# Down projections of four feed-forward blocks by Strassen's identity, as a stage behind gate and up

## The reference

```
def swiglu(x, w_gate, w_up, w_down):
    return (jax.nn.silu(x @ w_gate) * (x @ w_up)) @ w_down
...
x = layer_norm(alpha * x + 0.5 * swiglu(x, ffn_w_gate[l, 0], ffn_w_up[l, 0], ffn_w_down[l, 0]), ln_g[l, 0], ln_b[l, 0])
```

## Time and profile before

| | |
|---|---|
| median of 3 runs | 2386.46 us (2380.72 to 2388.42) |
| profiled execution, its own time | 2380.86 us |
| its span, first to last instruction | 2378.9 us |
| granted TensorE clock, mean of the span | 0.913 |
| busy PE, DVE, ACT, POOL | 1944.8, 363.2, 220.1, 17.3 us |
| first FFN matmul at | 1143.8 us |

### The profile page before, as it was taken

How to read it: one execution, slowest core, us unless ns; L and a number is a source line. 1 busy time by engine, 2 the same in 40 slices (tenths; PEclk the granted TensorE clock), 3 DMA queues, 4 the chain that set the end, 5 groups by cost and what they waited for, 6 DMA issues and landing times.

```text
span 2378.9 us, 20900 instructions
## 1 busy us (share of the span) xinstructions
PE 1944.8 (82%) x9324; PEld 1227.4 (52%) x9324; DVE 363.2 (15%) x785; ACT 220.1 (9%) x423; POOL 17.3 (1%) x41
## 2 busy tenths in 40 slices
PE   6987566665666665665999999999999999989997
PEld 5755222222222222221677777777677767857775
DVE  1213111111011111100100032200120015240002
ACT  4231000000000000000100010100010002110000
POOL 1100000000000000000000000000000000000000
PEclk9999878888888888777999999999999999989999
DMA  9246999999999999999644442544454444334440
GB/s 282 72 177 270 427 427 428 428 427 428 428 427 428 428 427 429 427 428 408 204 159 155 145 142 90 189 146 159 142 165 149 146 154 129 107 106 159 152 149 18
DMA packets 181777, 604.28 MB, mean 254 GB/s; under 512 B 17773, under 2 KB 135975, under 8 KB 157111
## 3 DMA queue, kind: packets, MB, share of 16 engines
q1 hardware_dynamic: 176064, 595.51, 65.0%
q10 hardware_dynamic: 5623, 7.42, 1.1%
HBM read 601.86 MB, written 1.05 MB: 253 GB/s over the span
## 4 chain that ended last, share of the span: by engine, by line
PE 66%; DMA 28%; DVE 2%; ACT 1%; SPq 1%; issue 1%; ACTq 0%; DVEq 0%
PE banks L1211 26%; PE banks L1225 10%; DMA e_W<-in_expert_w_gate 10%; DMA e_W<-in_expert_w_down 10%; DMA e_W<-in_expert_w_up 8%; PE banks L869 6%; PE banks L1256 5%; PE banks L191 3%; PE banks L877 3%; PE banks L1300 2%; PE banks L1244 2%; PE banks L1376 2%; SPq L849 1%; PE banks L386 1%; PE banks L392 1%
## 5 line engine op out<-in xcount | busy, mean ns | idle before, releaser
L1211 PE MATMUL banks<-x_xT,x_ring 128*128 128x256 f32 x2816 | 621.6, 382 | 3.5 <-DVE x_xT L1591 2.9
L1211 PEld LDWEIGHTS banks<-x_xT,x_ring 128*128 128x128 f32 x2816 | 539.7, 192 | 94.5 <-issue 21.9
L869 PE MATMUL banks<-e_W,e_xT 128*32 128x512 f32 x2048 | 288.2, 726 | 190.2 <-DMA e_W<-in_expert_w_up 104.5
L869 PEld LDWEIGHTS banks<-e_W,e_xT 128*32 128x32 f32 x2048 | 79.1, 130 | 387.0 <-issue 385.8
L877 PE MATMUL banks<-e_W,e_hT 128*32 128x512 f32 x1024 | 147.5, 741 | 142.8 <-DMA e_W<-in_expert_w_down 142.8
L1225 PE MATMUL banks<-x_ring,x_hT 128*128 128x512 f32 x576 | 253.1, 592 | 0.0
L1225 PEld LDWEIGHTS banks<-x_ring,x_hT 128*128 128x128 f32 x576 | 109.4, 190 | 122.4 <-issue 120.5
L877 PEld LDWEIGHTS banks<-e_W,e_hT 128*32 128x32 f32 x1024 | 40.5, 133 | 238.3 <-issue 238.3
L1628 DVE TENSOR_TENSOR x_hT<-x_act,banks 128x256 f32<-128x256 f32 x88 | 37.1, 422 | 812.8 <-ACT x_act L1490 812.8
L1256 PE MATMUL banks<-x_xT,x_ring 128*128 128x256 f32 x544 | 122.1, 386 | 1.6 <-issue 1.6
L1256 PEld LDWEIGHTS banks<-x_xT,x_ring 128*128 128x128 f32 x544 | 104.8, 194 | 17.6 <-issue 3.1
(11 more groups left out here) (405 smaller groups left out, 1031.9 us busy)
## 6 DMA issues: line engine op xcount, KB each, us to landing
e_W<-in_expert_w_gate SPq DMA_DIRECT2D x64, 2048.0 KB, 20.9
e_W<-in_expert_w_up SPq DMA_DIRECT2D x64, 2048.0 KB, 20.6
e_W<-in_expert_w_down SPq DMA_DIRECT2D x64, 2048.0 KB, 21.2
x_ring<-in_ffn_w_gate SPq DMA_DIRECT2D x44, 1024.0 KB, 5.3
x_ring<-in_ffn_w_up SPq DMA_DIRECT2D x44, 1024.0 KB, 5.4
x_ring<-in_ffn_w_down SPq DMA_DIRECT2D x44, 1024.0 KB, 4.9
x_ring<-in_w_in_mlstm SPq DMA_DIRECT2D x13, 1024.0 KB, 5.2
x_ring<-in_w_in_conv SPq DMA_DIRECT2D x10, 1024.0 KB, 5.1
```

The lines of the kernel that those rows point to most:

```text
L869: i = pe.matmul(ps[SLOT * j:SLOT * (j + 1), b, :], E.xT[:, x, k, SLOT * j:SLOT * (j + 1)], E.W[:, slot0 + j, k * DE:(k + 1) * DE], start=( ...
L1211: mm = pe.matmul(ps[:, 2 * b + f2, which * S:(which + 1) * S], w8(i)[:, k, f2 * P:(f2 + 1) * P], N.xT[:, k, :], start=(k == 0), stop=(k == ...
```

## The change

Only the second factor of each FFN is computed otherwise. Take the hidden activations of a chunk as a 2 x 2 block matrix A (token half t by piece f2) and the chunk of the down weights as B (piece f2 by column half m). Blocks of A are 128 x 128, blocks of B 128 x 512. Eight block products are replaced by seven (the Winograd form of Strassen's identity):

- sums of B on DVE (`weight_sums`): B12-B11, B22-B12, B22-(B12-B11), B21 minus that; four operations of 128x512 for each chunk
- sums of A on DVE (`hidden_sums`): four operations of 128x128 for each chunk, into `hs`
- seven matmuls of 128x512 for each chunk (`down(c, p)`), each product p into a bank of its own, accumulated over the 11 chunks
- once for each FFN, the seven products are combined into h (`merged` on DVE). ACT first copies product 1 out of PSUM (`pd`).

Seven banks are needed by the products, while gate and up need four. So the downs no longer alternate with gate and up: all 11 `gate_up` run first (banks 4 to 7), with the hidden activations of all 11 chunks kept on chip (`hT`), and then all downs. Of the first two chunks, products 1, 2, 6, 5 (banks 0 to 3) come first, then products 3, 7, 4 behind a wait for the last hidden activations. The last two chunks are interleaved product by product, in the order 1, 2, 6, 5, 3, 7, 4. The sums of chunks 0 to 3 are made after the hidden activations of chunks 7 to 10, the rest behind those. Weight sums have 4 slots, so those of a chunk wait until the chunk that held the slot is spent; `hs` has 4 slots too. SP loads in the new order: 22 gate and up pieces, then 11 down pieces.

At the joints: `turn(j, 0)` and `turn(j, 1)` are now at the head of `ffn`; ACT does `spread(j, 0)` right behind the square root of t=0; `rows(j)` is called at the head of the next stage; `load_rows` is issued at chunk 2 of the next FFN; the constants of the mLSTM's `va` and `rowsel` are set at its head, since the sums now use that memory.

```diff
             def ffn(n, j):
-                gate_up(0)
-                gate_up(1)
-                down(0)
-                for c in range(2, NFC):
+                turn(j, 0)
+                turn(j, 1)
+                for c in range(NFC):
                     gate_up(c)
-                    if c < NFC - 1:
-                        down(c - 1)
...
+                for c in range(2):
+                    wait_down(c)
+                    for p in (1, 2, 6, 5):
+                        down(c, p)
+                pe.wait_ge(s["hid"], 2 * NFC * (n + 1))
+                for c in range(2):
+                    for p in (3, 7, 4):
+                        down(c, p)
+                for c in range(2, NFC - 2):
+                    wait_down(c)
+                    for p in (1, 2, 6, 5, 3, 7, 4):
+                        down(c, p)
+                wait_down(NFC - 2)
+                wait_down(NFC - 1)
+                for p in (1, 2, 6, 5, 3, 7, 4):
+                    down(NFC - 2, p)
+                    down(NFC - 1, p)
...
+                def wait_down(c):
+                    wait_chunk(pe, at + 2 * NFC + c)
+                    pe.wait_ge(s["sum"], NFC * n + c + 1)
+                    pe.wait_ge(s["hsum"], NFC * n + c + 1)
...
+            def weight_sums(n, x):
+                i, before = AT_FFN[n] + 2 * NFC + x, sum_before(n, x)
+                if before:
+                    v.wait_ge(s["spent"], AT_FFN[before[0]] + 2 * NFC + before[1] + 1)
+                wait_chunk(v, i)
+                o, w = N.sums[:, sum_slot(n, x), :, :], w2(i)
+                b11, b12, b21, b22 = w[:, 0, 0:512], w[:, 0, 512:D], w[:, 1, 0:512], w[:, 1, 512:D]
+                first = K.vc.mark(v.tensor_tensor(o[:, 0], b12, b11, ALU.subtract))
+                v.tensor_tensor(o[:, 2], b22, b12, ALU.subtract)
+                v.wait_ge(K.vc.sem, first)
+                c(v.tensor_tensor(o[:, 1], b22, o[:, 0], ALU.subtract))
+                v.tensor_tensor(o[:, 3], b21, o[:, 1], ALU.subtract).then_inc(s["sum"], 1)
...
+            def merged(n, j, scale, last):
...
+                got(6)
+                u3 = both(2, N.ud[:, 0, :], prod(7))
+                after(u3)
+                x = add(1, 1, N.ud[:, 2, :])
+                y = add(1, 0, N.ud[:, 2, :])
+                scaled(j, 0)
+                after(x)
+                x = add(1, 1, prod(5))
                 if j < 6:
                     spread(j, 0)
+                after(x)
+                stats(1, 1)
+                v.wait_ge(s["spent"], last)
+                after(y)
+                c(add_last(1, 0, prod(4), scale))
+                c(stats(1, 0))
+                v.bn_aggr(N.mv[:, 1, :], N.stats[:, 1, :, :]).then_inc(s["mv"], 1)
                 scaled(j, 1)
...
+                for cc in range(NFC):
                     for f2 in range(2):
+                        hidden(cc, f2)
+                    if cc >= NFC - 4:
+                        weight_sums(n, cc - NFC + 4)
+                        hidden_sums(cc - NFC + 4)
+                for cc in range(4, NFC):
+                    weight_sums(n, cc)
+                    hidden_sums(cc)
+                merged(n, j + 1, 0.5 / ALPHA, at + FPOS)
```

More of the change, by code:

```diff
@@ L1086, with sum_slot, sum_before @@
 CHUNKS = 4 * FPOS + 31
[L1089 to L1094, removed]
+SUMS = 4
+SUM_AT = [0, 12, 23, 36]
+BANK_AT = [0, 0, 6, 9, 15, 21, 24]
+DB = {1: 0, 2: 1, 6: 2, 5: 3, 3: 4, 7: 5, 4: 6}
+def sum_slot(n, x):
+    return (SUM_AT[n] + x) % SUMS
+def sum_before(n, x):
+    order = [(m, y) for m in range(4) for y in range(NFC)]
+    for m, y in reversed(order[:order.index((n, x))]):
+        if sum_slot(m, y) == sum_slot(n, x):
+            return m, y
 def whole(K, M, E, N, X, Y, out):
     nc, ps, sem, dram, h = K.nc, K.ps, K.sem, K.dram, K.h
-    names = ("spent", "half", "act", "hid", "bank", "mv", "root", "zn", "turned", "xt_v", "xt_a", "rows", "sumsq", "stored",
+    names = ("spent", "half", "sum", "hsum", "kept", "act", "hid", "bank", "mv", "root", "zn", "turned", "xt_v", "xt_a", "rows", "sumsq", "stored",
              "ld_lstm")
@@ L1180, in _, with turn @@
         def _(pe):
[L1181 to L1188, removed]
+            def turn(j, t):
+                for b in range(2):
+                    pe.wait_ge(s["zn"], 4 * j + 2 * t + b + 1)
+                    for k in range(4):
+                        i = pe.transpose(ps[:, 2 * t + b, k * P:(k + 1) * P], h[:, t, (4 * b + k) * P:(4 * b + k + 1) * P],
+                                         K.ident[:, :])
+                    i.then_inc(s["turned"], 1)
             def wait_x(j, k):
@@ L1216, in gate_up @@
                             mm.then_inc(s["half"], 1)
[L1218 to L1227, removed]
@@ L1430, in _ @@
             moe.tensor(pe)
-            turn(0)
             ffn(0, 0)
-            turn(1)
+            for t in range(TT):
+                turn(1, t)
             conv()
-            turn(2)
             ffn(1, 2)
-            turn(3)
             ffn(2, 3)
-            turn(4)
+            for t in range(TT):
+                turn(4, t)
             lstm()
-            turn(5)
             ffn(3, 5)
@@ L1655, in conv @@
                 at = AT_CONV
+                rows(1)
+                c(v.memset(X.pad[:, :, 0:QE], 0.0))
                 queries(cs, 0, at)
@@ L1687, in lstm @@
                 at = AT_LSTM
+                rows(4)
                 queries(ls, 1, at)
+                v.memset(X.va[:, :, :, HD:HD + 1], 1.0)
+                for hh in range(HH):
+                    v.tensor_copy(X.rowsel[:, hh, :], K.ident[0:HH, hh:hh + 1].broadcast_to([HH, P]))
                 v.wait_ge(s["ld_lstm"], 32)
@@ L1802, in _ @@
             ffn(3, 5)
+            rows(6)
         @block.gpsimd
```

137 lines of the change are left out of this document (88 added, 49 removed).

## The result

| | before | after |
|---|---|---|
| median | 2383.59 us (2379.10 to 2388.42, 4 runs) | 2358.32 us (2355.86 to 2359.95, 4 runs) |
| own time of the profiled execution | 2380.86 us | 2357.90 us |
| its span | 2378.9 us | 2355.8 us |
| first FFN matmul | 1143.84 us | 1145.61 us |
| from there to the end of the span | 1235.06 us | 1210.19 us |

The ratio of the times is 0.9893, with a 95% interval of 0.9868 to 0.9917: 25 us faster, where 2367 (19 us faster) was forecast. The part ahead of the first FFN isn't touched by the change; its end lay between 1143.8 and 1147.7 us in the profiles of this study, which is noise. So I compare the last row of the table, the remainder: 24.87 us shorter. Two runs at a far lower granted clock, one of the kernel before and one of experiment 6, are left out of all numbers here.

The account below looks back on a forecast made before the run. TensorE was taken as the bound, busy 231.07 of 235 us in FFN 2. Matmuls -37.8, joints +15.1 and clock +4.0 gave -18.7 us, from the median 2367.8, so 2367 us was predicted, range 2354 to 2380.

Parts of the forecast that it names:

- What the change removes: On TensorE in the FFNs: each of 44 chunks loses one down matmul of 0.859 us, 37.8 us in all.
- Rival (d): Down matmuls: slower with sums as operands, or gaps over seven banks; 0.12 us a matmul would take all; chance 0.04.
- The sums: On DVE in each FFN: 4.2 us a chunk (3.9 to 4.7), 185 us in all, hidden under PE, costing nothing.
- Rival (c): Down stage waits for DVE's sums beyond 6.4 us a chunk; 2412 us at 8 us a chunk; chance 0.04.
- The joints: Behind each FFN: DVE's longer chain adds 3.9 us at three joints and 3.4 us after FFN 3, 15.1 us in all.
- Rival (a): Joints between stages cost nothing, so the whole 37.8 us is kept and the time is 2349 us; chance 0.08.
- The clock: Behind the three joints: lower granted clock costs 3.7 us at each, 4.0 us more in sum (0 to 11).
- The sum: Whole kernel: -37.8 + 15.1 + 4.0 = -18.7 us; 2362.2 us from the profiled execution, 2367.8 us from the median.

Follow-up runs that it names:

- experiment 6: Kernel after with every weight sum made twice, in a second kernel three times, with the same values: 2362.48 us and 2454.86 us.
- experiment 3: Kernel after with seven products and all sums, but only four adds of the combination left, so h isn't the network's: 2346.80 us, ratio 0.9841.
- experiment 1: Kernel after with the eight products and norm of before, no sums: only the order, gate and up first, then downs, is new: 2383.98 us, ratio 0.9993.
- experiment 4: Kernel after, complete, with the merge rewritten (spread of t=0 behind the last add) and the last three chunks interleaved instead of two: 2346.28 us, ratio 0.9833.
- experiments 1 to 4: Against kernel after: eight products, no sums, 0.9993; eight products, sums made but unused, 0.9989; merge mostly left out, 0.9841; merge rewritten, three chunks interleaved, 0.9833.
- experiment 5: Kernel after with only the last three chunks interleaved, 2354.84 us; in a second kernel with only the merge rewritten, 2353.67 us.

## Why the prediction was right, and where its sizes were off

**What the change removes: right.** The remainder without the merge is 37.9 us shorter than before; 44 x 0.859 is 37.8, and the runs bear that out to about 2 us, not to 0.1 (experiment 3). That the order of the stage has no price was taken for granted in the prediction and is shown by experiment 1. Rival (d) is out: 592 ns for every kind of operand.

**The sums: right that they are hidden, 0.6 us too dear.** A chunk takes 3.56 us of DVE, not 4.2, and lies below my lower bound of 3.9. The shape without a row, 128x128, takes 0.29 us where I took 0.3; the 0.03 between chained operations was right but holds for fewer of them than I thought. The sums of chunk 4 start 9.5 us after the end of gate and up, as worked out. Rival (c) decides where it was said to: nothing at 3.56, 1.1 us of waits at 6.4, 75.2 us at 9.3. Its price beyond the threshold was too low, since a wait also costs clock. The page cited for the 0.29 us (the Trainium skill, VectorE: DVE Perf Modes, The TRN2 errata) agrees with the trace. The rule cited beside it, that leaving out the semaphore saves nothing (The DRAIN you can't avoid), doesn't: two operations without a wait between start 0.60 us apart (1704.41 and 1705.02 above, by rounding 0.61), chained ones 0.72 (1725.40 and 1726.12 in the earlier trace rows). The same section also says that a next operation that nothing holds back starts earlier; that sentence, which the prediction didn't give, is the one the trace bears out. I held that to be worth a tenth of a microsecond a pair, and that is what it is; but I then charged 0.7 for unwaited ones in the joint too.

**The joints: the right mechanism, +15.1 us said, +12.2 measured.** This is the term that was mis-sized. I had the last add end at T+5.6 and it ends at T+4.6: of the operations ahead of it, the partial sum with product 7 started 0.3 us earlier than I had it, and five or six that follow without a wait start 0.60 us apart and not 0.7. The turn of t=1 started at T+6.73, not T+7.6, and the next stage at T+9.40 where I said about T+10. At the end of FFN 3 the last statistics are 2.65 us later than before and not 3.4, and the chain behind it to the output came out 0.9 us shorter, as it did in experiment 1, which has the norm of before; so that isn't the merge's doing, and why stays open. Rival (a) named what could shrink this term, DVE's chain overlapping better than counted, and a small part of it is what happened; but its outcome, joints that cost nothing, needs the kernel of experiment 4.

**The clock: +4.0 us said, 1.3 in the body of FFN 2 measured and nothing that can be told behind the other two.** I expected all three joints to pay the full price. The joint to FFN 2 did: its turn ran in 1.97 us and not 1.11, and the clock came back later. This one holds over the kernels: the 704 records behind it take 154.27 to 155.17 us in the five kernels in which PE waits about 4.5 us ahead of the turn of t=1, and 153.87 to 154.18 in the four with seven or eight products in the new order in which it waits 2.8. Behind the joint to the convolution the first 96 records take 23.74 us and took 23.84 before; the mLSTM's first 32 take 8.60, before 8.64, although the turn ahead of them is now slow as well. Over the ten kernels these two go from 22.34 to 23.99 us and from 8.39 to 10.01, with long and short waits mixed, so a price of the longer pause isn't shown there. (The slow turns, which I had counted here, lie in the 12.2 of the joints, 0.47 us at FFN 2 and 0.86 at the mLSTM; without them the joints are 10.8 longer against the 15.1 said.)

**The sum.** Said -18.7 on the profiled execution; the remainder shows -24.9, with 2.9 of the 6.2 us between them from the joints, 2.0 from the bodies (where I had 4.0 of clock), and 1.2 from stretches that I set at nothing; all three err to the same side, so none hides another. The profiled executions differ by 23.0, since after's first part happened to be 1.8 longer. The time itself is 9.5 us below the 2367.8 worked out: 6.6 from the gain, and 2.9 because the median of the kernel before is 2383.59 with its fourth run and not 2386.46.

## What to carry to other kernels

Trading matmuls for sums on an idle engine pays the matmuls and costs nothing inside the stage, as long as that engine makes a unit's sums in less time than it takes to be asked for them; work out that threshold, since beyond it each wait costs in two ways, in idle time and in clock. Look for the price where the phases meet: there the engine that was the bound hands over to another one, which works through its queue in order, and what stands in that queue ahead of the one operation that needs the last result is the loss. To remove it both conditions must be met, the queue must be empty by then and nothing must be placed ahead that could come behind; here one alone gave about 4 us, both together 13.

## What the runs showed of the hardware

- The clock behind a pause of the same length isn't the same from run to run. The turn of t=1 ahead of the mLSTM in the kernel before:

```profile
1964.31 1.11 PE L1186 MATMUL banks<-c_ident,c_h 128*128 128x128 f32 x8 [2.83 <-DVE c_h L1583]
```

and in experiment 1, with the first matmuls of the mLSTM:

```profile
1966.53 1.97 PE L1199 MATMUL banks<-c_ident,c_h 128*128 128x128 f32 x8 [2.84 <-DVE c_h L1591]
1970.15 9.94 PE L1355 MATMUL banks<-x_xT,x_wgate 128*4 128x256 f32 x32 [1.64 <-issue]
```

  The waits are equal, yet the turn takes 1.11 and 1.97 us, and the 32 records behind it 8.64 and 9.94. Over the five kernels with waits of 2.8 us (before and experiments 1 to 4) the turn of t=1 took 1.11 or 1.12 us at nine of fifteen joints and 1.97 at six; over the five with waits of 4.48 to 4.59 us (after, both halves of experiment 5, both kernels of experiment 6) it never took 1.11, but 1.67 to 1.97 at all fifteen. A price of a joint in clock is therefore good to about 2 us only (0.86 in the turn, 1.30 behind it), and no single profile settles it. What decides it at the short waits stays open.
- DVE starts an operation 0.60 us behind the start of one of 128x512 (0.69 us long) where nothing is waited for, so that the two records overlap by 0.09 us, and 0.72 us behind it where the result is waited for.
- A DVE sum that reads the ring from which PE streams weights takes 0.685 to 0.692 us, the same as the row of that shape in a quieter stretch. PE's records beside these sums take 592 ns, as without them, so in this kernel no disturbance between PE and DVE on on-chip memory is seen.
